# One layer of a two-block network on one core: the two up-projections interleaved tile by tile, with one wait ahead of both

## The reference

```python
attn = nsa_attention(...)                       # (1, 512, 512)
rnn = rg_lru_branch(xr, gr, ...)                # (1, 512, 1024): a scan over the 512 positions
merged = sigmoid(g_a) * (attn @ w_up_attn) + sigmoid(g_b) * (rnn @ w_up_rnn)
x = x + merged @ w_out
hn = rms_norm(x, norm2_w)
x = x + square(relu(hn @ mlp_w1)) @ mlp_w2
```

## Time and profile before

| | |
|---|---|
| median of 3 runs | 2738.23 us (2737.07 to 2745.19) |
| time of the profiled execution | 2738.23 us |
| its span, first to last instruction | 2736.4 us |
| PE busy | 2413.0 us, 88% of the span |
| mean granted clock of PE | 0.937 of full |
| mean DMA rate over the span | 202 GB/s; 426 GB/s in most of the last third |

### The profile page before, as it was taken

One profiled execution on the slowest core, in us unless ns is written; L12 is line 12 of the kernel. 1 busy time (PEld: TensorE's weight loads), 2 busy tenths in 40 slices (PEclk: granted clock), 3 DMA queues, 4 the chain that ended last, 5 costly groups with the idle time before them and its releaser, 6 DMA issues.

```text
span 2736.4 us, 20853 instructions
## 1 busy us (share of the span) xinstructions
PE 2413.0 (88%) x8572; PEld 1141.3 (42%) x8572; DVE 602.8 (22%) x1213; ACT 330.5 (12%) x638; POOL 169.0 (6%) x156
## 2 busy tenths in 40 slices
PE   7998989899989999997998998698788888888875
PEld 3654444454444554443664444433233333333332
DVE  1243352423053323002252112211000000000003
ACT  2012221311021110002101001000000000000001
POOL 0000000000004330000000000000000000000001
PEclk9998999899999999998978999799999999999898
DMA  6210101002122222212722333599999999999995
GB/s 244 81 58 3 59 5 58 16 31 107 77 108 95 110 73 109 92 62 74 121 87 92 117 122 139 235 426 426 426 426 427 426 427 426 425 424 425 418 416 193
DMA packets 69089, 553.09 MB, mean 202 GB/s; under 512 B 20960, under 2 KB 25184, under 8 KB 37440
## 3 DMA queue, kind: packets, MB, share of 16 engines
q1 hardware_dynamic: 41952, 513.92, 46.2%
q10 hardware_dynamic: 16816, 25.32, 3.0%
q0 software_dynamic: 10224, 12.48, 1.4%
HBM read 544.95 MB, written 35.68 MB: 212 GB/s over the span
## 4 chain that ended last, share of the span: by engine, by line
PE 63%; DMA 19%; DVE 6%; ACT 2%; issue 1%; ACTq 1%; DVEq 0%; POOL 0%; POOLq 0%
PE ps L374 23%; DMA sb<-in_eu 14%; PE ps L832 10%; PE ps L656 8%; PE ps L429 6%; PE ps L862 5%; DMA sb<-in_eg 2%; PE ps L548 2%; PE ps L716 1%; PE ps L518 1%; PE ps L540 1%; DMA sb<-in_ed 1%; DVE sb L1237 1%; PE ps L519 1%; PE ps L635 1%
## 5 line engine op out<-in xcount | busy, mean ns | idle before, releaser
L374 PE MATMUL ps<-sb 128*128 128x512 f32 (+2 forms) x1920 | 789.9, 573 | 17.5 <-DVE sb L1716 5.3
L832 PE MATMUL ps<-sb 128*64 128x512 f32 x2048 | 487.9, 632 | 102.9 <-DMA sb<-in_eu 71.3
L374 PEld LDWEIGHTS ps<-sb 128*128 128x128 f32 x1920 | 359.8, 195 | 431.1 <-issue 413.4
L832 PEld LDWEIGHTS ps<-sb 128*64 128x64 f32 x2048 | 178.2, 144 | 390.7 <-issue 366.8
L862 PE MATMUL ps<-sb 128*64 128x512 f32 x992 | 241.0, 642 | 33.0 <-DMA sb<-in_ed 17.7
L429 PE MATMUL ps<-sb 128*128 128x512 f32 x512 | 251.3, 621 | 0.0
L656 PE MATMUL ps<-sb 128*128 128x512 f32 x512 | 220.0, 592 | 0.5 <-issue 0.5
L862 PEld LDWEIGHTS ps<-sb 128*64 128x64 f32 x992 | 77.7, 146 | 174.8 <-issue 155.4
L656 PEld LDWEIGHTS ps<-sb 128*128 128x128 f32 x512 | 97.2, 190 | 122.8 <-issue 122.8
L1237 DVE TENSOR_TENSOR sb<-sb 128x32 f32<-128x32 f32 (+11 forms) x261 | 107.1, 428 | 133.8 <-PE ps L622 83.2
L429 PEld LDWEIGHTS ps<-sb 128*128 128x128 f32 x512 | 93.1, 199 | 80.2 <-issue 79.7
(11 more groups left out here) (252 smaller groups left out, 1508.7 us busy)
## 6 DMA issues: line engine op xcount, KB each, us to landing
sb<-in_eg SPq DMA_DIRECT2D x64, 2048.0 KB, 32.8
sb<-in_eu SPq DMA_DIRECT2D x64, 2048.0 KB, 33.8
sb<-in_ed SPq DMA_DIRECT2D x62, 2048.0 KB, 33.9
sb<-in_m SPq DMA_DIRECT2D x16, 2048.0 KB, 7.4
sb<-in_winF SPq DMA_DIRECT2D x6, 2048.0 KB, 9.8
sb<-in_mg SPq DMA_DIRECT2D x8, 1536.0 KB, 6.2
sb<-in_mgg SPq DMA_DIRECT2D x4, 2048.0 KB, 7.4
sb<-in_wo SPq DMA_DIRECT2D x4, 2048.0 KB, 7.2
```

The lines of the kernel that those rows point to most:

```text
L374: ins = pe.matmul(out, lhsT, rhs, start=k == 0, stop=k == len(pieces) - 1)
L832: ins = pe.matmul(o[64 * e:64 * e + 64, :], x[:, k, 64 * e:64 * e + 64], weight(2 * mat + e)[:, 512 * k:512 * k + 512], start=k == 0, stop ...
```

## The change

The weights of both up-projections are packed into one array `mgy`, which for each m holds the 4 pieces of `ya m` followed by the 8 of `yr m`. It is loaded as four groups of two m each (1536 KB instead of 2048 KB a transfer), into slots 1, 2, 1, 2. PE now does `ya 0`, `yr 0`, `ya 1`, `yr 1`, and so on; the wait for `rnn` at 8 stands ahead of all of them. The banks start at 0. DVE takes the tiles out in the same new order. The slots 1 and 2 of `wo1` and of `m1` are exchanged.

```diff
-        plan += [(("mya", 0), 1), (("myr", 0), 2), (("myr", 1), 1), (("wo1", 0), 2), (("wo1", 1), 1)]
-        plan += [(("m1", g), (2, 1, 0)[g % 3]) for g in range(8)] + [(("m2", g), g % 3) for g in range(8)]
+        plan += [(("mgy", g), 1 + g % 2) for g in range(4)] + [(("wo1", 0), 1), (("wo1", 1), 2)]
+        plan += [(("m1", g), (1, 2, 0)[g % 3]) for g in range(8)] + [(("m2", g), g % 3) for g in range(8)]
...
             for j in range(4):
                 pe.wait_ge(*T.free("o", j))
-            ring = [T.at[("gr", 7)][0] + 1]
+            pe.wait_ge(S("rnn"), 8)
+            ring = [0]
...
-            pe.wait_ge(*loaded("mya", 0))
-            w = slot("mya", 0)
             for m in range(8):
+                w = slot("mgy", m // 2)
+                at_ = 1536 * (m % 2)
                 o = open_tile(pe, ("ya", m), any_bank())
-                chain(o, [(w[:, 512 * m + 128 * k:512 * m + 128 * k + 128], attnT[:, k, :]) for k in range(4)], ("ya", m))
-            W.ended[("mya", 0)] = ("ya", 7)
-            pe.wait_ge(S("rnn"), 8)
-            for m in range(8):
-                w, at_ = slot("myr", m // 4), 1024 * (m % 4)
+                pe.wait_ge(*loaded("mgy", m // 2))
+                chain(o, [(w[:, at_ + 128 * k:at_ + 128 * k + 128], attnT[:, k, :]) for k in range(4)], ("ya", m))
                 o = open_tile(pe, ("yr", m), any_bank())
-                pe.wait_ge(*loaded("myr", m // 4))
-                chain(o, [(w[:, at_ + 128 * k:at_ + 128 + 128 * k], GR[:, k, :]) for k in range(8)], ("yr", m))
-                W.ended[("myr", m // 4)] = ("yr", m)
+                chain(o, [(w[:, at_ + 512 + 128 * k:at_ + 640 + 128 * k], GR[:, k, :]) for k in range(8)], ("yr", m))
+                W.ended[("mgy", m // 2)] = ("yr", m)
...
-            for n, name in enumerate(("ya", "yr")):
-                for m in range(8):
-                    g = GT[n][:, m, :]
-                    dve.wait_ge(*T.free("gate", 2 * m + n))
+            for m in range(8):
+                g0, g1 = GT[0][:, m, :], GT[1][:, m, :]
+                dve.wait_ge(*T.free("gate", 2 * m))
+                dve.wait_ge(*T.free("gate", 2 * m + 1))
+                for g, name in ((g0, "ya"), (g1, "yr")):
                     dve.wait_ge(*T.full(name, m))
                     dve.scalar_tensor_tensor(g, g, 1.0, T.ap(name, m), ALU.add, ALU.mult).then_inc(T.s(name, m), 1)
...
-            load(("mya", 0), A["mya"])
-            for g in range(2):
-                load(("myr", g), A["myr"][:, 4096 * g:4096 * g + 4096])
+            for g in range(4):
+                load(("mgy", g), A["mgy"][:, 3072 * g:3072 * g + 3072], 3072)
```

More of the change, by code:

```diff
@@ L2308, in host @@
                               2).reshape(128, -1)
-    o["mya"] = ft(g["w_up_attn"][0][heads]).reshape(128, -1)
-    o["myr"] = ft(g["w_up_rnn"][0]).reshape(128, -1)
+    o["mgy"] = np.concatenate([ft(g["w_up_attn"][0][heads]).reshape(128, 8, -1), ft(g["w_up_rnn"][0]).reshape(128, 8, -1)],
+                              2).reshape(128, -1)
     o["wo1"] = halves(g["w_out"][0])
@@ L2383, in host @@
     return {k: np.ascontiguousarray(v) for k, v in o.items()}
-_INS = ["x", "sm", "ck", "rw", "rb", "winF", "winN", "lru", "cw1", "mgg", "mya", "myr", "wo1", "m1", "m2", "fn1", "bb", "cc", "z2", "dft", "glu",
+_INS = ["x", "sm", "ck", "rw", "rb", "winF", "winN", "lru", "cw1", "mgg", "mgy", "wo1", "m1", "m2", "fn1", "bb", "cc", "z2", "dft", "glu",
         "mg2", "wo2", "gf", "fn2", "eg", "eu", "ed"]
```

## The result

Over 16 runs each, the changed kernel takes 2753.17 us in the median (2745.20 to 2758.78) and the kernel before 2737.40 us (2725.96 to 2745.19): a ratio of 1.0058, 95% interval 1.0047 to 1.0069, which is 15.8 us slower. Twelve further runs of the changed kernel lie between 2742.96 and 2762.14 us, with a median of 2754.4. The profiled execution took 2755.23 us with a span of 2753.4, 17.0 us more than the one of before.

What follows compares the result with a forecast made beforehand. PE was taken to bound the kernel at the changed place, with no idle time between gr 7 and the end of yr 7. 15.1 us wait plus 2.0 us clock on 2738.2 gave 2755.3 us, range 2749.5 to 2762.

Steps and rivals of the forecast that it cites:

- The wait: Ahead of ya 0, behind gr 7: PE idles from 625.25 until rnn reaches 8 at 640.32, +15.1 us.
- The clock: Behind that idle time: about 4 us at 1.2 GHz, +2.0 us, bounds 0 to 3.9.
- The clock rule: PE after idle gaps: clock falls to half rate; rows said to agree, drop after 17.92 us, none after 2.27.
- The drop behind the wait for POOL: At wo1, behind 2.26 us of waiting: low clock costing 1.9 us, kept in the forecast, possibly missing after the change.
- B: PE's stage from the start of wo1 to the transposes, 62.65 us before; forecast added nothing there.
- stage A: PE from the last 20 gate-tile instructions to the start of wo1, 93.50 us before; forecast's 17.1 us falls here.
- The banks: ya 0 in bank 0, yr 0 in bank 1, which DVE frees by 632.6, before rnn is at 8: 0.
- The loads: mgy groups land in 6.2 us; mgy 2 and mgy 3 have 14 us to spare: 0.
- the rival of the late load: Third and fourth mgy groups take 20 us, each holding PE some 6 us: 2767 us, chance 0.03.
- What comes behind: After the changed stage: later loads start from PE's ends, so nothing absorbs the shift of 17 us.
- The two rivals in which it is given back: State-space matmuls at full clock return 19 us: 2736 us, 0.04; transfers in the last third absorb the delay: 2738 us, 0.03.
- The two on the wait itself: At ya 0: rnn ready earlier, 2740 us, 0.01; low clock for all 82.6 us, costing 82 us, at most 0.01.

Runs made afterwards that it cites:

- e2: Kernel before, with only the wait for rnn at 8 moved from ahead of yr 0 to ahead of ya 0: 2750.41 us, ratio 1.0054.
- e4: Changed kernel with 17 unread matmul calls ahead of the wait for rnn, keeping PE at work in the idle time: 2753.77 us, ratio 1.0061.
- e1: Changed kernel with the wait for rnn moved behind ya 0, ahead of yr 0: 2748.29 us, ratio 1.0042.
- e3: Changed kernel with ya 0 to 3 first, then the wait for rnn, yr 0 to 3, then pairs: 2740.85 us, ratio 1.0009.
- e7: Changed kernel run again unaltered, on another chip: 2754.88 us, ratio 1.0066.
- e5: As e3, but the ring of banks starts at 2 as before the change, not at 0: 2735.55 us, ratio 0.9993.
- e6: Kernel before, but the first tile of wo1 and wo2 waits for one more merged tile ahead of each of its 8 calls: 2726.56 us, ratio 0.9965.
- e8: Kernel of e4 run again, beside e7 on one chip: 2753.22 us, ratio 1.0061.

## Why the prediction was right

It said 2755.3 us, and 2753.17 was measured; 17.1 us more were forecast, 15.8 came. By its steps:

- **The wait**: 15.1 us forecast, 15.27 us in the profile, released by DVE's last recurrent product as said, and e2 shows that this one wait carries the change. The small excess is the restart, 0.37 us behind the release where less than 0.1 was forecast.
- **The clock**: 2.0 us forecast from the restart at 1280, within 0 to 3.9. It was 85.20 - 82.56 = 2.64 us, and 2.53 us against e4's 82.67. The mechanism was right, the term a little small: the low clock lasted 5.2 us instead of 4.
- **The clock rule**: the Trainium skill (TensorE: Matmul & The Clock Gate, Why this matters for your kernels) says that an idle array falls back to half rate. The long waits agree: low clock behind 15.27 us in the changed kernel, 11.54 in e1 and 3.77 in e3. The short ones go both ways: waits of about 2.2 us lost nothing in the changed kernel and 1.7 us in the kernel before. When the prediction let its rows agree with "none after 2.27 us", it left out that its own row of 2.26 us had lost 1.9, which it counted only further down. The lower bound of 0 rests on a row that doesn't repeat: at the same place e7 lost 1.7 us.
- **The drop behind the wait for POOL**: the forecast kept it and named its absence as a loss of 1.9 us less. It was absent, B is 1.7 us shorter. With it the sum of the stages is 18.0 - 1.7 = 16.3 us, nearer to what was measured than the forecast. So the total of 17.1 owes a little to luck: stage A was forecast 0.9 us too low, B 1.7 us too high. How often the kernel before has this drop isn't known from its one profile. That it comes and goes isn't due to the change: it is absent in e2 too, in the old order, and there again in e1 (62.55 us).
- **Tiles, DVE, POOL**: 0, as measured. The wait for POOL went from 2.26 to 2.18 us.
- **The banks**: 0 is right for this kernel, but only because the wait for `rnn` covers the one for bank 1. The prediction saw the cover (bank 1 free at 632.6, before `rnn`) but didn't price the bank without it; e3 shows 3.77 us of idle time and 1.6 us of clock, and e5, where 1.22 us then go to `rnn`, gets 4.0 us of that back.
- **The loads**: `mgy 2` was asked for at 662.54 (663.0 forecast) and `mgy 3` at 683.14 (683.6). No wait for them, so the rival of the late load fell.
- **What comes behind**: the shift stays. The two rivals in which it is given back fell: the state-space matmuls again took 40.58 us at low clock, and the stream of expert weights started 15.7 us later and ended later. The two on the wait itself fell too: `rnn` came no sooner with PE idle, and the low clock ended after 5.2 us.

State-space matmuls in the changed kernel:

```profile
1418.36 40.58 PE L713 MATMUL ps<-sb 128*128 128x64 f32 x192 [3.48 <-DVE sb L1699]
```

## What to carry to other kernels

Before moving a wait forward in an engine's list, count the work that stands between its old and its new place and doesn't need it: that work was the cover, and here 27.5 us of it had hidden a branch that was 15 us late. A wait for the last of many pieces can be put ahead of the call that reads that piece; in e6, with a chain of eight calls, this took away two idle times of 2.26 and 1.65 us. And a resource that costs nothing behind a long wait must be priced again when that wait is shortened.

## What the runs showed of the hardware

The same wait can be followed by a low clock in one profile and not in the next: behind the wait for POOL, 2.26 us in the kernel before and 2.18 us in e1 cost 1.7 and 1.6 us, and 2.18 to 2.25 us cost nothing in the changed kernel, e2, e3, e4, e5, e7 and e8. It happens to one and the same kernel: ahead of the 304 instructions that stand before `wo2`, the changed kernel and its repeat e7 both waited 2.26 us, and only e7 lost 1.7 us.

```profile
1519.13 130.73 PE L374 MATMUL ps<-sb 128*128 128x512 f32 x304 [2.26 <-DVE sb L1719]
```

```profile
1517.92 132.43 PE L374 MATMUL ps<-sb 128*128 128x512 f32 x304 [2.26 <-DVE sb L1719]
```

A third such place is the second half of the 64-column matmuls, behind a wait of about 0.8 us for a transfer. In the changed kernel it ran at low clock and in e2 at full clock, with a like wait:

```profile
1365.27 11.55 PE L676 MATMUL ps<-sb 128*128 128x64 f32 x64 [0.80 <-DMA sb<-mbi_d]
```

```profile
1360.22 7.36 PE L679 MATMUL ps<-sb 128*128 128x64 f32 x64 [0.62 <-DMA sb<-mbi_d]
```

From there to the start of the state-space matmuls the first took 53.1 us and the second 48.9. The length of the wait doesn't tell the two apart: behind 0.69 us the clock was low in e8 and full in e6, and behind 1.07 us in e3 it was full.

```profile
1356.46 11.60 PE L678 MATMUL ps<-sb 128*128 128x64 f32 x64 [0.69 <-DMA sb<-mbi_d]
```

```profile
1344.07 7.36 PE L682 MATMUL ps<-sb 128*128 128x64 f32 x64 [0.69 <-DMA sb<-mbi_d]
```

What decides it isn't shown here. So a single profile of this kernel says no more than some us about its total, while stage A, at the edit, repeats to a tenth.
